# A two-layer MoE trunk in float32: additions in two groups, the first pair picked by products, the weight ring in pieces shared by both experts of a pair

## The reference, cut to what matters

```python
D_MODEL = 1024; SEQ = 512; DEPTH = 2
N_EXPERTS = 32; EXPERT_FF = 512; TOP_K_IN_GROUP = 2

def expert_block(args):
    xb, e = args
    g, u = jnp.split(xb @ w_gate_up[e], 2, axis=-1)
    return (jax.nn.silu(g) * u) @ w_down[e]

for i in range(DEPTH):
    xn = rms_norm(h, norm_mix[i])
    mix = sliding_window_attention(xn, ...) if i == 0 else gated_short_conv(xn, ...)
    h = h + mix
    h = h + hierarchical_moe(rms_norm(h, norm_ffn[i]), ...)   # gate-weighted sum of two experts a token
return rms_norm(h, final_norm)
```

## Time and profile before

| what | value |
|---|---|
| time, median of 3 runs | 1353.9 us (1350.97 to 1355.2) |
| the profiled execution: its own time | 1351.3 us |
| its span, from first to last instruction | 1349.4 us |
| mean granted TensorE clock | 0.988 of full |
| PE busy | 1294.5 us, 96% of the span |
| DVE, ACT, POOL busy | 43%, 19%, 8% |
| DMA bytes | 450.73 MB, 334 GB/s over the span |
| experts, layer 0 | first product 199.27 us, last down products from 649.50 us |
| experts, layer 1 | first product 875.35 us, last down products from 1325.38 us |
| busy share of the 16 DMA engines in these stretches | 9 (90% or more) in the page's tenths |

### The profile page before, as it was taken

One profiled execution on the slowest core, in us unless ns is written; L12 is line 12 of the kernel. 1 busy time (PEld: TensorE's weight loads), 2 busy tenths in 40 slices (PEclk: granted clock), 3 DMA queues, 4 the chain that ended last, 5 costly groups with the idle time before them and its releaser, 6 DMA issues.

```text
span 1349.4 us, 14705 instructions
## 1 busy us (share of the span) xinstructions
PE 1294.5 (96%) x5986; PEld 668.7 (50%) x5986; DVE 578.0 (43%) x1232; ACT 256.7 (19%) x556; POOL 110.4 (8%) x120
## 2 busy tenths in 40 slices
PE   7999989999999999999999999899999999999996
PEld 5777653344334444333588888633443333443332
DVE  5586342343343333333566661423433433433334
ACT  3257611010100111000532221110101001101002
POOL 3850010000000000000000000100000000000000
PEclk8999989999999999999999999899999999999998
DMA  9301768999999999999723337589999999999993
GB/s 346 97 1 52 307 279 357 427 427 428 426 425 427 426 426 427 426 428 428 213 94 105 113 149 294 221 342 426 427 427 427 427 426 425 427 426 426 426 428 150
DMA packets 65306, 450.73 MB, mean 334 GB/s; under 512 B 17722, under 2 KB 33108, under 8 KB 40660
## 3 DMA queue, kind: packets, MB, share of 16 engines
q1 hardware_dynamic: 58976, 436.09, 78.0%
q0 software_dynamic: 5760, 12.59, 2.5%
q10 hardware_dynamic: 500, 1.06, 0.2%
HBM read 451.79 MB, written 6.32 MB: 339 GB/s over the span
## 4 chain that ended last, share of the span: by engine, by line
PE 83%; DMA 10%; DVE 4%; ACT 1%; issue 1%; DVEq 0%; SPq 0%; ACTq 0%
PE ps L1155 29%; PE ps L943 20%; PE ps L1180 15%; PE ps L1147 9%; DMA big<-in_moe_w_gate_up_dram 7%; DMA small<-in_moe_w_gate_up_dram 2%; PE ps L1128 2%; PE ps L1086 1%; PE ps L901 1%; PE ps L1121 1%; PE ps L1025 1%; PE ps L1141 1%; PE ps L992 1%; ACT arena L795 1%; DVE h L1726 1%
## 5 line engine op out<-in xcount | busy, mean ns | idle before, releaser
L1155 PE MATMUL ps<-big,arena 128*64 128x512 f32 x1200 | 464.8, 597 | 5.1 <-DMA big<-in_moe_w_gate_up_dram 1.9
L1747 DVE TENSOR_TENSOR h<-ps,h 128x512 f32<-128x512 f32 x240 | 154.7, 686 | 203.7 <-PE ps L1147 203.7
L1155 PEld LDWEIGHTS ps<-big,arena 128*64 128x64 f32 x1200 | 133.5, 136 | 144.4 <-issue 143.2
L1180 PE MATMUL ps<-small,arena 128*64 128x512 f32 x336 | 152.7, 597 | 3.3 <-ACT arena L795 3.1
L1155 PE MATMUL ps<-small,arena 128*64 128x512 f32 x336 | 152.7, 597 | 1.1 <-DMA big<-in_moe_w_gate_up_dram 1.1
L1147 PE MATMUL ps<-arena_parts 128*128 128x512 f32 x512 | 151.4, 419 | 1.7 <-DVE arena_parts L1710 1.7
L1147 PEld LDWEIGHTS ps<-arena_parts 128*128 128x128 f32 x512 | 86.6, 188 | 95.6 <-issue 83.8
L943 PE MATMUL ps<-xt_parts,small_parts 128*128 128x512 f32 x288 | 111.5, 397 | 2.9 <-DVE big_parts L1839 2.9
L790 ACT ACTIVATE gain<-ps,slot_root 128x512 f32<-128x512 f32 x32 | 22.0, 688 | 477.9 <-PE ps L1155 477.9
L943 PE MATMUL ps<-xr_parts,small_parts 128*128 128x512 f32 x272 | 106.6, 392 | 0.0
L943 PE MATMUL ps<-xt_parts,big_parts 128*128 128x512 f32 x256 | 99.7, 389 | 0.0
(11 more groups left out here) (208 smaller groups left out, 1646.6 us busy)
## 6 DMA issues: line engine op xcount, KB each, us to landing
big<-in_moe_w_gate_up_dram SPq DMA_DIRECT2D x75, 2048.0 KB, 22.9
small<-in_moe_w_gate_up_dram SPq DMA_DIRECT2D x21, 2048.0 KB, 21.7
small<-in_moe_w_down_dram SPq DMA_DIRECT2D x21, 2048.0 KB, 24.7
arena<-in_moe_w_gate_up_dram SPq DMA_DIRECT2D x11, 2048.0 KB, 22.0
xr<-in_moe_w_down_dram SPq DMA_DIRECT2D x11, 2048.0 KB, 23.7
xt<-in_moe_w_down_dram SPq DMA_DIRECT2D x11, 2048.0 KB, 23.3
arena<-in_moe_w_down_dram SPq DMA_DIRECT2D x11, 2048.0 KB, 24.6
xr<-in_moe_w_gate_up_dram SPq DMA_DIRECT2D x11, 2048.0 KB, 22.4
```

What stands on the lines that cost most here:

```text
L1155: mm = nc.tensor.matmul(ps[2 + half][j * BLOCK:(j + 1) * BLOCK, :], xg[:, k, j * BLOCK:(j + 1) * BLOCK], ws[j][:, k % FT, half * FF:(half ...
L1180: mm = nc.tensor.matmul(ps[6 + c][j * BLOCK:(j + 1) * BLOCK, :], hidT[:, k, j * BLOCK:(j + 1) * BLOCK], ws[j][:, k, c * HALF:(c + 1) * HAL ...
L1747: ins = V.tensor_tensor(hs, ps[c][:], hs, ALU.add)
```

## The change: what it does

1. **Ring pieces.** Piece c = 0 to 3 is now two of the eight row blocks of gate_up of both experts, and c = 4, 5 two of the four row blocks of down of both. Each is loaded by two DMAs of 1 MB (one for each expert), with 8 KB in one stretch for each partition instead of 16 KB. A quarter of gate_up needs one piece. `gu_done` counts after every quarter, the new `first_done` and `down_done` after each half of the down products, so places come free one at a time.
2. **Additions in two groups.** Tiles 0 and 1 of the pair before are formed together after the second quarter, in banks 0/1 and 6/7, and tiles 2 and 3 after the third.
3. **The tail of a pair.** `turn_picked` stands between the last quarter and `index`; `down` is one unbroken run, and it is called with pieces 4 and 5, so both are waited for before its first product. On DVE `take` stands before `find_pair`.
4. **The first pair.** A comparison on DVE forms `first_sel`, and PE multiplies h with it (`pick_first`, 32 products), which gives the rows of the first pair already turned. No gather, no row numbers and no transposes for pair 0. What they needed (`index`, `turn_ranks`, `count`) moves behind its second quarter (`first_indexes`), and the second pair's indexes with it.
5. **After layer 0.** DVE does the low parts of the first weight blocks between the two halves of the last additions; PE turns half 1 only after two of the eight k of the first convolution tile. The order on ACT is not changed.
6. **At the end.** POOL multiplies h by the gain for tiles 0 and 1 of the last norm, and DVE then only scales. `value_load` of the fullest expert and its branch stand ahead of the last additions.
7. Three semaphores are merged into others (`rel_in`, `w_o_in`, `eps_ready`).

```diff
                 def load(n):
                     i, c = divmod(n, PIECES)
-                    if c < 4:
-                        w = w_gate_up[l, 2 * i + c % 2].rearrange("(p k) n -> p k n", p=P)[:, c // 2 * FT:(c // 2 + 1) * FT]
-                    else:
-                        w = w_down[l, 2 * i + c - 4].rearrange("(p k) n -> p k n", p=P)
-                    sp.dma_start(ring[l][n % RING], w).then_inc(ring_in[n % RING], 16)
+                    w = w_gate_up if c < 4 else w_down
+                    k = 2 * (c if c < 4 else c - 4)
+                    for j in range(2):
+                        sp.dma_start(ring[l][n % RING][:, 2 * j:2 * j + 2],
+                                     w[l, 2 * i + j].rearrange("(p k) n -> p k n", p=P)[:, k:k + 2])\
+                            .then_inc(ring_in[n % RING], 16)
...
                     if used < 4:
-                        sp.wait_ge(main.gu_done, 2 * (l * PAIRS + before) + used // 2 + 1)
+                        sp.wait_ge(main.gu_done, 4 * (l * PAIRS + before) + used + 1)
+                    elif used == 4:
+                        sp.wait_ge(first_done, l * PAIRS + before + 1)
                     else:
                         sp.wait_ge(main.down_done, 2 * (l * PAIRS + before + 1))
...
                 for i in range(PAIRS):
                     n = l * PAIRS + i
-                    gather(S, l, n, i % AHEAD, 2 * n if i else None)
+                    if i:
+                        gather(S, l, n, i % AHEAD, 2 * n)
+                    else:
+                        pool.wait_ge(S.index_ready, n + 1)
...
+            def pick_first(S, l):
+
+                pe.wait_ge(first_selected, l + 1)
+                for k in range(DT):
+                    for t in range(TT):
+                        mm = nc.tensor.matmul(ps[k // 4][:, k % 4 * P:(k % 4 + 1) * P],
+                                              h[:, t, :].rearrange("p (q k) -> p k q", k=DT)[:, k, :], first_sel[:, t, :],
+                                              start=(t == 0), stop=(t == TT - 1))
+                    if k % 4 == 3:
+                        mm.then_inc(S.picked_turned, 1)
+
+            def first_indexes(S, l):
+
+                o = l * PAIRS
+                pe.wait_ge(S.selected, o + 1)
+                pe.wait_ge(tab_ready, l + 1)
+                index(S)
+                turn_ranks()
+                count(l)
+                pe.wait_ge(S.selected, o + 2)
+                index(S)
+                pe.wait_ge(ranks_taken, l + 1)
...
                 for i in range(PAIRS):
                     n = o + i
                     pe.wait_ge(S.rows_taken, 2 * n + 1)
-                    ws = weights(i, 0)
-                    gate_up(both((0, 1)), ws)
+                    gate_up(both((0, 1)), weights(i, 0)).then_inc(S.gu_done, 1)
+                    gate_up(both((2, 3)), weights(i, 1)).then_inc(S.gu_done, 1)
                     if i == 0:
-                        pe.wait_ge(ranks_taken, l + 1)
+                        first_indexes(S, l)
                     spread(S, n, i)
                     if i:
-                        add_pair(i - 1, 0)
+                        add_tiles(i - 1, (0, 1))
                     pe.wait_ge(S.rows_taken, 2 * n + 2)
-                    gate_up(both((2, 3)), ws).then_inc(S.gu_done, 1)
+                    gate_up(both((4, 5)), weights(i, 2)).then_inc(S.gu_done, 1)
                     if i:
-                        add_pair(i - 1, 1)
-                    ws = weights(i, 2)
-                    gate_up(both((4, 5)), ws)
-                    if i:
-                        add_pair(i - 1, 2)
-                    last_quarter(S, ws)
-                    if i:
-                        add_pair(i - 1, 3)
+                        add_tiles(i - 1, (2, 3))
+                    last_quarter(S, weights(i, 3))
+                    if i < LAST:
+                        if i:
+                            pe.wait_ge(S.added, l * ADDS + TT * (i - 1) + 3)
+                        pe.wait_ge(S.picked_in, 16 * (l * LAST + i + 1))
+                        turn_picked(S)
...
                     turn_hidden(S, n)
-                    ws = weights(i, 4)
-                    down_first(S, n, ws)
-                    if i < LAST:
-                        if i:
-                            pe.wait_ge(S.added, l * ADDS + TT * i)
-                        pe.wait_ge(S.picked_in, 16 * (n + 2))
-                        turn_picked(S)
-                    down_last(S, n, ws)
+                    down(S, n, weights(i, 4), weights(i, 5))
...
-            for half in range(2):
-                for t in range(TT):
-                    turn_half(t, half)
+            for t in range(TT):
+                turn_half(t, 0)
...
                         if k == 0:
                             pe.wait_ge(xt_even, TT * 3)
+                        if k == 2:
+                            for t in range(TT):
+                                turn_half(t, 1)
...
+            pool.wait_ge(gain_in, 16 * 2)
+            for t in range(2):
+                pool.wait_ge(h_ready, 2 * (TT + t + 1))
+                nc.gpsimd.tensor_tensor(xr[:, t, :], h[:, t, :], gain[:], ALU.mult).then_inc(pool_scaled, 1)
...
+                if i == 4 and t < 2:
+                    dve.wait_ge(pool_scaled, t + 1)
+                    V.tensor_scalar(xr[:, t, :], xr[:, t, :], rstd[:, t:t + 1], None, ALU.mult).then_inc(xr_ready, 1)
+                    return
```

More of the change, by code:

```diff
@@ L1284, in experts @@
                                 pe.wait_ge(over_in[l], (q + 1) * 64)
[L1285 to L1287 removed]
+                                ws = lambda j, k: big[:, j, k, :]
+                                gate_up(both((0, 1, 2, 3, 4, 5)), ws)
+                                last_quarter(O, ws)
                                 turn_hidden(O, q)
[L1289 to L1291 removed]
+                                ws = lambda j, k: small[:, j, k, :]
+                                down(O, q, ws, ws)
                                 pe.wait_ge(over_masked[l], q + 1)
@@ L1687, in take, with hidden @@
                         .then_inc(S.rows_taken, 1)
-            def hidden(S, n, slot=0):
+            def hidden(S, n, slot=0, per=1):
                 dve.wait_ge(S.silu_ready, n + 1)
-                dve.wait_ge(S.gu_done, 2 * n + 2)
+                dve.wait_ge(S.gu_done, per * (n + 1))
                 for half in range(2):
@@ L1740, in experts, with add_tile @@
                 take(S, o)
+                dve.wait_ge(S.indexed, o + 1)
+                find_pair(S, 0)
+                select(S, slice(2, 4))
+                dve.wait_ge(rank_ps, 2 * l + 2)
+                step(V.tensor_reduce(most_f[:], ps[7][:, 0:E], X, ALU.max))
+                V.tensor_copy(fullest[:, l:l + 1], most_f[:]).then_inc(route_ready, 1)
+                dve.wait_ge(S.indexed, o + 2)
+                find_pair(S, 1)
                 dve.wait_ge(h_stored, 16 * TT * (l + 1))
-                def add_pair(i, t):
+                def add_tile(i, t, bank):
                     dve.wait_ge(S.combined, before + TT * i + t + 1)
@@ L1785, in experts, with conv_begin @@
                         for c in range(2):
-                            add_last(count + 2 * t + c + 1, t, c)
-                dve.wait_ge(h_ready, 2 * TT * (l + 1))
+                            add_last(before + ADDS + 2 * t + c + 1, t, c)
+                def conv_begin(between_halves):
+                    split_low_of(CONV_SPLIT, 0, [0])
+                    for t in range(TT):
+                        take_turned(2, t, [0])
+                    split_low_of(CONV_SPLIT + 1, 0, [1])
+                    between_halves()
+                    for k in (2, 3):
+                        split_low_of(CONV_SPLIT + k, 0, [k])
+                    for t in range(TT):
+                        take_turned(2, t, [1])
+                    for k in range(FT, DT):
+                        split_low_of(CONV_SPLIT + k, 0, [k])
                 dve.wait_ge(route_ready, l + 1)
```

179 lines of the change are left out of this document (81 added, 98 removed).

## The result

The changed kernel takes 1376.03 us (median of 4 runs, 1374.25 to 1377.8), the kernel before 1352.97 beside it: ratio 1.017, 95% interval 1.0148 to 1.0192. Slower, and outside the range 1343 to 1367 that was forecast.

What follows compares the result with a forecast made beforehand. The weight stream was taken to bound the experts of both layers. Layer 0 0.0, convolution +2.8, layer 1 +1.2 and tail -0.4 gave +3.6 on 1351.3, so 1354.9; with 2.6 for the median 1357.5 us, range 1343 to 1367.

Steps and rivals of the forecast that it cites:

- The bound: Experts of both layers: they end when the weight stream ends, and PE's own time is worth nothing until it is later.
- PE's saving: Steady pair of experts: fewer re-entries save PE 0.6 us a pair, 28.64 to about 28.0, hidden by the stream's 30.3.
- the 1.0 us behind the last landing: End of layer 0's experts: down started 1.0 us behind the last landing, taken as slack for a later stream.
- -7.5 and -6.4 us at the stream's start: First refill: starts 7.5 us earlier in layer 0, 6.4 in layer 1, through quicker picking and an earlier freed place.
- The bound that I gave for this step: Picking for the first pair: at half clock it would last 7.1 us longer than the 7.1 forecast, the upper bound.
- Pace of the stream: Expert weight stream: 8 KB packets cost 0.08 us a piece, +6.9 us a layer (0 to 9.4).
- The rival that 8 KB packets cost nothing: Expert weight stream: 8 KB packets cost what 16 KB ones do, time 1344 us; chance 0.20, faster.
- small transfers are dear: Rival, expert weight stream: 8 KB packets as dear as 4 KB, 28 us a layer; 1378 with half; chance 0.05, slower.
- The last down: End of each layer's experts: its start moves 0.0 us in layer 0, +1.2 in layer 1; its length changes by 0.
- The convolution: Start after layer 0: half 1 turned later delays ACT's copies and DVE's split, second weight tile +2.8 us.
- The tail: Last norm: value_load off the path and a shorter DVE step give -0.4 us, between -1.9 and +0.6.
- Gather of pair 1: Inside the stream now: +0.7 us, PE waits 0 to 4.9, gap in the stream 0.7 (0 to 3.2).

Runs made afterwards that it cites:

- e3: Kernel before, with each 2 MB piece loaded by two 1 MB DMAs, 8 KB in one stretch; 1365.64 us, ratio 1.0109.
- e5: Changed kernel, with the second down piece waited for only before its own half of the down products; 1368.06 us.
- e10: Changed kernel with the edits of e5, e6 and e7 together; 1349.92 us, ratio 0.9969.
- e11: e10 with the 14 middle pairs' pieces as in the kernel before (2 MB, one DMA, 16 KB stretches); 1347.81 us, ratio 0.9951.
- e8: Changed kernel, with only half of each piece loaded from the tenth piece of a layer on; 1341.70 us.
- e9: Kernel before, with only half of each piece loaded from the tenth piece of a layer on; 1347.49 us.
- e1: Changed kernel, with picking reading 128 neighbouring columns of h as weights instead of every eighth; 1357.75 us, ratio 1.0036.
- e2: Changed kernel, with each place loaded by one 2 MB DMA over both experts, still 8 KB in one stretch; 1375.68 us.
- e4: Changed kernel, with both halves of h turned ahead of the convolution's products again; 1369.47 us.
- e6: Changed kernel, with first_sel as the weights in picking, h moving in 512-column rows, then copied by ACT and turned by PE; 1362.86 us, ratio 1.0069.
- e7: Changed kernel, with ACT's squares and roots put ahead of its copies of the turned half 1 at the convolution's start; 1371.39 us.
- e12: Changed kernel, without POOL's multiplications by the gain; DVE forms all four tiles of the last norm; 1374.24 us.

## Why the prediction was wrong

- **The bound: right.** "The experts of either layer end when the stream ends": in every run but the half-byte ones the chain of both layers has a landing of the stream in the last two pairs. In the change it is the last piece; in others, e3, e5, e10 and e11 among them, it is an earlier one, with PE's own work behind it. PE's saving (0.6 a pair forecast, 0.72 measured) is worth nothing in the change, and 8 us a layer in e8 against e9. One reading in it was wrong: the 1.0 us behind the last landing was not slack that a later stream could use up. In the chain of before PE waits for a gate_up piece of the last pair, which lands at 628.9, and works 20.5 us to the last down; in e3 the last landing of layer 0 is 5.9 us later and the last down 5.8.
- **The step that failed: "32 products of 128 columns are 64 records. Eight such records take 0.89 us, 0.111 each, so 7.1 us".** Measured 15.48, 0.242 each. The eight records of the row have weights side by side; those of `pick_first` take every eighth column of h. So -7.5 and -6.4 us at the stream's start were -0.1 and, counted from the choice of the first pair in layer 1, +1.4: 15 of the 23 us that the sum is off. The bound that I gave for this step (7.1 longer, by the clock) was of nearly the right size for another reason, but it stood outside the range, which added only the packets and the gather to the upper side. The Trainium skill had the warning: page "SBUF — State Buffer", section "Door 1: The DMA port swizzle", says that SBUF is read in 16-byte lines and that an access which goes to a new line each time pays for it. With weights 32 bytes apart every one does; e1 agrees, 0.334 against 0.192 us. The trace of before had a hint too: the weight loads of `turn_picked`, with the same stride, take 0.194 us, those of L936, without, 0.140.
- **Pace of the stream: right.** 0.08 a piece forecast, 0.079 measured; 9.2 us from first to last landing in layer 0 with the gather and the gaps, where 6.9 + 1.4 were forecast. In layer 0 pieces land 5.16 us apart on average, 5.13 forecast. The rival that 8 KB packets cost nothing is out by e3. That the number of DMAs costs is out by e2. The Trainium skill, page "DMA: Bandwidth & Descriptors", section "Bandwidth", gives a 1 MB transfer 78% of peak, which could be read that way; the traces don't agree, since the queue of 1 MB DMAs moved 420 GB/s and half as many DMAs gave 4.973 us a piece for 4.975. The rival "small transfers are dear" named 1378 us with half of its price, close to the 1376 measured; that is a coincidence, since its sign, 0.12 us a piece and more, did not come.
- **The last down: missing.** I let its start move and kept its length. In the profiled execution PE runs it, behind its wait, at a clock of 0.66 in the first 5 us: 1.5 and 1.6 us, and 1.7 more behind the wait at the second convolution tile. 4.8 us in all. The one in layer 1 varies: the last down there took 7.10 us in e2, e4, e6, e7 and e12, and 10.08 in e1.
- **The convolution: right in place and mechanism,** +4.2 instead of +2.8, since the 18 products ran partly at half clock (5.98 us for 4.1). The sum had a slip as well: C+30.8 less C+28.1 is 2.7. With ACT's order matched, in e7, PE waits no longer at the second tile.
- **The tail: the right size for the wrong halves.** -0.4 forecast, -0.1 measured: -1.0 and +0.8, as e12 shows. Here the Trainium skill's page "SBUF — State Buffer", section "Who interferes with whom", which I had put at the upper end, is borne out: 2.52 us beside GpSimd, 0.75 alone.
- **Gather of pair 1: no finding.** It is issued at 214.14; PE turns those rows at 222.1 without a wait. With quicker picking the wait that I had bounded at 4.9 us comes: 2.15 us in layer 0 of e10, 0.65 in layer 1 of e1.

With e1's edit alone the time is 1357.75, beside the forecast of 1357.5. That is luck. By the spans of the profiled executions e1 is 9.1 us above the kernel before, where +3.6 was forecast: its last downs took 8.79 and 10.08 us (+4.7), the second tile to the choice +1.8, C to the second tile 1.4 more than forecast, against 1.3 and 1.2 less for the two stretches up to the last downs. Its profiled execution, 1360.29, was the slowest of seven, and the median lies 2.5 below it.

## What to carry to other kernels

A product's price has two parts, what moves and what is loaded as weights; take it from a row whose weights have the same stride, or add the stride as a bound of its own. Where a stream is the bound, its first free place and its last landing set the time: shorten what stands ahead of the one and behind the other (e6, e5), and expect nothing from work saved between. When a change makes PE wait, let the lower clock behind the wait enter the range (0 to 3.0 us for a run of down products here), and look for the engine whose order was left as it was.

## What the runs showed of the hardware that I had not expected

- In picking, a 128x128 float32 weight load took 0.192 us with weights side by side and 0.334 with weights 32 bytes apart; records came 0.116 and 0.242 us apart.
- 8 KB packets cost the stream 0.077 to 0.079 us for each 2 MB against 16 KB ones (426 and 420 GB/s), whether a place was filled by one DMA or by two.
- Behind nine waits for DMA of 2.1 to 4.0 us in the change's experts, TensorE's granted clock over the next 5 us was 0.51 to 0.70 four times and 1.00 five times; the down products behind them took 8.6 to 9.5 us or 7.1. It was 0.57 from 674 to 678 in the convolution's first tile. Values between are mixtures of the two levels, 1.2 and 2.4 GHz.
- A DVE scaling of 128x1024 float32 took 0.75 us alone and 2.52 beside a GpSimd product of the same tile size.
